# A fused streaming-encoder block on eight cores: the constant matmuls at the opening taken out, and the last tile's residual added on VectorE

## What is computed

```
h    = rms_norm(x, ln_mix_pre)
B, C, u, v = split(h @ w_in)                       # 2048 -> 4096
y_a  = per-head-norm(B * conv3_causal(C * u))      # 1024 channels
y_b  = per-group-norm(pool(v) @ pool_w) * scale    # 1024 channels
x    = x + rms_norm(concat(y_a, y_b) @ w_out, ln_mix_post)
hf   = rms_norm(x, ln_ffn_pre)
ff   = (silu(hf @ w_gate) * (hf @ w_up)) @ w_down  # 2048 -> 5632 -> 2048
out  = x + rms_norm(ff, ln_ffn_post)
```

## Time and profile before

| | us |
|---|---|
| median of three runs | 2515.8 |
| the three runs | 2512.62, 2515.8, 2649.74 |
| the profiled execution, its own time | 2530.27 |
| its span on the slowest core (core 1) | 2528.7 |
| spans of the eight cores | 2506.2 to 2528.7 |

### The profile page before, as it was taken

How to read it: one execution, slowest core, us unless ns; L and a number is a source line. 1 busy time by engine, 2 the same in 40 slices (tenths; PEclk the granted TensorE clock), 3 DMA queues, 4 the chain that set the end, 5 groups by cost and what they waited for, 6 DMA issues and landing times.

```text
span 2528.7 us, 31891 instructions; the slowest of 8 cores (2506.2 to 2528.7 us)
## 1 busy us (share of the span) xinstructions
PE 2460.2 (97%) x11570; PEld 1110.1 (44%) x11570; DVE 1056.3 (42%) x1614; ACT 641.0 (25%) x1184; POOL 219.0 (9%) x373
## 2 busy tenths in 40 slices
PE   6999999999999999999999999999999999999994
PEld 2444444444444444444444444444444444444441
DVE  4445627544445543322235552654545445200202
ACT  3222334222222222311123333432222222111110
POOL 0000000000000000002101000000000000000212
PEclk7889999999999999999999999999999999999997
DMA  8859768988998998776987524896554445344664
GB/s 214 162 77 126 144 197 219 187 137 126 135 134 127 134 134 215 243 231 183 256 148 112 96 84 167 225 193 116 91 92 84 84 88 92 129 150 150 182 194 66
DMA packets 75339, 374.53 MB, mean 148 GB/s; under 512 B 8240, under 2 KB 10544, under 8 KB 45872
## 3 DMA queue, kind: packets, MB, share of 16 engines
q0 software_dynamic: 54160, 313.55, 62.4%
q1 hardware_dynamic: 21024, 58.94, 7.3%
HBM read 509.82 MB, written 65.01 MB: 227 GB/s over the span
## 4 chain that ended last, share of the span: by engine, by line
PE 94%; DMA 3%; DVE 2%; issue 0%; SPq 0%; POOL 0%; ACT 0%; DVEq 0%; POOLq 0%; ACTq 0%
PE bank L409 92%; DMA unit<-wst_gu 1%; PE bank L600 1%; DMA F<-xt 1%; PE bank L449 1%; PE bank L872 1%; DMA unit<-wst_in 0%; DVE XG L444 0%; DVE unit L441 0%; PE bank L401 0%; DVE XG L441 0%; SPq L499 0%; PE bank L531 0%; POOL yT L1118 0%; DVE F L444 0%
## 5 line engine op out<-in xcount | busy, mean ns | idle before, releaser
L409 PE MATMUL bank<-XG,unit 128*128 128x512 bf16 x7680 | 1698.9, 383 | 11.5 <-DMA unit<-wst_in 6.7
L409 PEld LDWEIGHTS bank<-XG,unit 128*128 128x128 bf16 x7680 | 756.3, 99 | 937.4 <-issue 88.0
L409 PE MATMUL bank<-F,unit 128*128 128x512 bf16 x3072 | 669.2, 379 | 0.0
L409 PEld LDWEIGHTS bank<-F,unit 128*128 128x128 bf16 x3072 | 300.6, 98 | 362.4
L441 DVE TENSOR_TENSOR tt<-tt 128x512 f32<-128x512 f32 (+1 forms) x152 | 104.9, 691 | 597.8 <-ACT tt L438 576.8
L435 ACT ACTIVATE tt<-bank 128x512 f32<-128x512 f32 x228 | 136.2, 597 | 481.5 <-PE bank L409 474.8
L441 DVE TENSOR_TENSOR bank<-bank,tt 128x512 f32<-128x512 f32 x152 | 106.3, 699 | 357.5 <-PE bank L409 357.5
L438 ACT ACTIVATE tt<-bank 128x512 bf16<-128x512 f32 (+1 forms) x160 | 95.0, 595 | 492.7 <-PE bank L409 483.8
L441 DVE TENSOR_TENSOR unit<-unit 128x1024 bf16<-128x1024 bf16 x304 | 196.1, 686 | 10.4 <-PE bank L409 2.1
L441 DVE TENSOR_TENSOR F<-bank,tt 128x512 bf16<-128x512 f32 x138 | 95.2, 691 | 118.2 <-PE bank L409 97.3
L357 POOL DMA_DIRECT2D unit<-wst_gu x100 | 52.9, 529 | 1016.8 <-PE bank L409 913.0
(11 more groups left out here) (74 smaller groups left out, 874.3 us busy)
## 6 DMA issues: line engine op xcount, KB each, us to landing
unit<-wst_gu POOLq DMA_DIRECT2D x100, 1024.0 KB, 10.6
unit<-wd_bf POOLq DMA_DIRECT2D x64, 1024.0 KB, 5.5
unit<-wo_bf POOLq DMA_DIRECT2D x32, 1024.0 KB, 6.5
unit<-wst_in POOLq DMA_DIRECT2D x31, 1024.0 KB, 12.0
unit<-wd_bf POOLq DMA_DIRECT2D x32, 768.0 KB, 6.6
wd_bf<-wst_dn POOLq DMA_DIRECT2D x32, 704.0 KB, 15.8
tt<-xt SPq DMA_DIRECT2D x64, 256.0 KB, 6.2
yT<-XG POOLq DMA_DIRECT2D x56, 256.0 KB, 9.6
```

Of the source, the lines that this page charges most:

```text
L409: inst = e.matmul(out, lhsT=pairs[n][0], rhs=pairs[n][1], start=(start and n == 0), stop=(stop and n == nk - 1), skip_group_check=lax)
```

## The change

Opening: the memset of `tt8` and the 24 matmuls are gone. End, for the last tile only: `dn_tile` gets `apart=True`, with which `Acc` closes its running sum at the fifteenth square and leaves the sixteenth out of it; `rsqrt` sums both over partitions, with two matmuls into one bank. Items 0 to 5 stay as they were. Items 6 to 15 are done by the new `item_here`: VectorE scales the chunk and adds x to it, and SP stores the sum with a plain transfer. For this x after the mixing is read back from `yT` into F0, chunks 6 to 15, in five pieces.

```diff
         class Acc:
-            def __init__(self, n, tile=2, home=None):
-                self.n, self.i, self.tile, self.home = n, 0, tile, home
+            def __init__(self, n, tile=2, home=None, apart=False):
+                self.n, self.i, self.tile, self.home, self.apart = n, 0, tile, home, apart
+                self.last = None
...
                 q = self.q
-                if self.i < self.n:
+                if self.apart and self.i == self.n:
+                    self.last = q
+                    return
+                if self.i < self.n - self.apart:
                     tt(Tt[self.tile][:], Tt[self.tile][:], sqv(q), ALU.add, [self.h, q], [self.h])
...
             def rsqrt(self, n, out, hout):
                 b = next_bank()
-                P.op("pe", lambda e: e.matmul(banks[b.i][:], lhsT=ones[:], rhs=self.outv(), start=True, stop=True),
+                P.op("pe", lambda e: e.matmul(banks[b.i][:], lhsT=ones[:], rhs=self.outv(), start=True, stop=self.last is None),
                      reads=[self.out, "ones"], writes=[b])
+                if self.last is not None:
+                    stat_mm(b, self.last, False, True)
                 rsqrt_to(b, n, out, hout)
...
+            def item_here(self, i):
+                t = self.t
+                p = t % 2
+                stt(ffv(p, i), ffv(p, i), C_G3 + i, Tt[3][:], Kff(p, i) + [self.h], Kff(p, i))
+                tt(xs(i), ffv(p, i), xs(i), ALU.add, Kff(p, i) + Kx(i), Kx(i))
+                P.dma("sp", lambda e: e.dma_start(out=yT[t][:, i, :], in_=xs(i)).then_inc(sems[f"oh{i}"], 16),
+                      f"oh{i}", reads=Kx(i), writes=[("y", t, i)])
...
-        P.op("dve", lambda e: e.memset(Tt[8][:], 0.0), writes=[("sq", 2), ("sq", 3)])
...
-        warm = next_bank()
-        for i in range(24):
-            P.op("pe", lambda e: e.matmul(banks[warm.i][:], lhsT=ones[:], rhs=Tt[8][:].bitcast(BF16)[:, 0:TT], start=True, stop=True),
-                 reads=["ones", ("sq", 2)], writes=[warm])
...
+                if c2 == 3 and p == 1:
+                    for n in range(3, 8):
+                        P.dma("sp", lambda e, n=n: e.dma_start(out=xs2(n), in_=yT[to][:, 2 * n:2 * n + 2, :]).then_inc(sems[f"xl{n}"], 16),
+                              f"xl{n}", reads=[("y", to, 2 * n), ("y", to, 2 * n + 1)], writes=Kx2(n))
...
-            acc = dn_tile(1, side_d1)
+            acc = dn_tile(1, side_d1, p == 1)
             tail = Tail(to, acc)
 
         tail.rs3()
-        for i in range(KC):
+        for i in range(6):
             tail.item(i)
-        names = [f"o{q}" for q in range(16)] + [f"{x}{q}" for x in ("xo", "xp") for q in range(8)]
+        for i in range(6, KC):
+            tail.item_here(i)
+        names = [f"o{q}" for q in range(16)] + [f"oh{q}" for q in range(6, 16)] + [f"{x}{q}" for x in ("xo", "xp") for q in range(8)]
         P.wait_all("sp", [(q, P.dma_cnt[q]) for q in names])
```

More of the change, by code:

```diff
@@ L151, in build_program @@
     sem_names = (list(ENGS) + [f"u{i}" for i in range(5)] + [f"xl{i}" for i in range(8)] + [f"xm{i}" for i in range(8)] + [f"xp{i}" for i in range(8)]
-                 + [f"xo{i}" for i in range(8)] + [f"o{i}" for i in range(16)] + ["ua0", "ua1", "ua2", "ua3", "misc", "pw", "xhl", "st4", "st5", "st6", "st9", "st7", "rs0", "rs1"]
+                 + [f"xo{i}" for i in range(8)] + [f"o{i}" for i in range(16)] + ["ua0", "ua1", "ua2", "ua3", "oh6", "oh7", "oh8", "oh9", "oh10", "oh11", "oh12", "oh13", "oh14", "oh15", "misc", "pw", "xhl", "st4", "st5", "st6", "st9", "st7", "rs0", "rs1"]
                  + [f"cv{i}" for i in range(4)])
@@ L1074, in gu_fast, with dn_tile @@
                 side(n)
-        def dn_tile(par, side):
-            acc = Acc(KC)
+        def dn_tile(par, side, apart=False):
+            acc = Acc(KC, apart=apart)
             pend = []
```

## The result

The changed kernel's median is 2498.5 us (2497.5 to 2500.4, four runs). The two runs of the kernel before that they are compared with took 2512.6 and 2515.8 us; the ratio is 0.9938, 95% interval 0.9914 to 0.9962.

A forecast was written before the change was run, and what follows sets the result against it. The kernel was taken as matmul-filled, its end bound by transfers, then by VectorE; opening 0, end -9.5 us (0.8 from the last sum included) and reload 0 gave 2506.3 us from the 2515.8 us median, range 2500 to 2521 us.

The forecast's parts named there:

- Opening: 0: Opening: removing the memset and 24 constant matmuls changes nothing, because the weight transfer covers any slower start; 0 us.
- The rule that the prediction cites against the change: Opening: the Trainium skill says TensorE's clock is throttled by default and activity releases it, so the phase would start at half speed.
- all-cold bound: Opening: with the clock at 1.2 GHz throughout, the first phase ends at 34.2 us; core 1 loses nothing, core 0 0.7 us.
- Rival (b): Opening: it stays cold into the next phase; up to 5 us lost where cover fails, 2507 to 2511 us; chance 0.10.
- Rival (c): Opening: slow matmuls leave PE no gap, so the clock is up afterwards; gain about 2 us, 2504 us; chance 0.06.
- The last sum: 0.8 us: End: the last square in its own matmul takes VectorE's add and hand-over off the chain; 0.8 us saved.
- That is 1.53 us an item and 15.3 us for ten.: End: VectorE's scale and dependent add for items 6 to 15, so VectorE ends 7.8 us later than before.
- 2.3 us remain for SP's last waits and the end of the program: End: time from the last landing, at about 2526.4 us, to the end of the old span at 2528.7 us.
- The transfers as not the bound (17.0 against VectorE's 19.3 us): End: six accumulating transfers at 1.66 us and ten stores at 0.70 us, together 17.0 us, finish before VectorE's path.
- Rival (a): End: plain stores are as dear as accumulating transfers; only 0.8 us saved, 2515.0 us; chance 0.08.
- Rival (d): End: VectorE's ten scale-and-add pairs are slow; at 3.06 us an item 5.8 us slower, 2521.6 us; chance 0.03.
- Rival (e): Whole program: saving as forecast, but the median falls on an execution with the 0.81 clock; 2520.8 us; chance 0.11.

The follow-up runs named there:

- e10: The full change measured again beside the kernel before: 2499.0 us against 2512.3 us, ratio 0.9952.
- e1: Only the opening edit (memset and 24 constant matmuls removed) on the kernel before, with its old end: 2512.9 us against 2512.3 us, ratio 0.9993.
- e8: The full change plus 20 extra matmuls in PE's wait for the second weight unit: 2498.4 us, the kernel before 2513.0 us.
- e7: The full change with the order turned round, ten VectorE items first and six accumulating ones last: 2508.2 us against 2513.0 us for the kernel before.
- e12: The full change with each of the ten scales issued one item ahead: 2502.8 us against 2513.6 us for the kernel before, ratio 0.9952.

## Why the prediction was wrong, point by point

The mechanism was right and two sizes were off. The saving at the end was forecast as 9.5 us and is 11.9 us. The base to carry it to was 2515.8 us, and the kernel before runs at 2512.3 us. With both put right the forecast would have been 2500.4 us instead of 2506.3 us; 2498.5 to 2499.0 us is measured. Of the last 1.4 to 1.9 us, 0.5 us is that the slowest core stands less above the mean (e10); the rest is open.

- **Opening: 0.** Right, by the reason given: e1's mean span is that of before within 0.2 us, and the weight unit ends PE's wait. The rule that the prediction cites against the change is borne out too: without the constant matmuls the first pair takes 1.06 us on every core. With them it took 0.59 us on seven of eight cores of before, so core 1, from which the prediction argued, was the exception. The all-cold bound wasn't reached on any core of e1; the latest end of the phase was 32.3 us, against the bound's 34.2 us. Rival (b) falls with it. Rival (c), a clock that is up behind the wait, did not come by itself, and brought about on purpose (e8) it gave no gain clear of the spread.
- **The last sum: 0.8 us.** Measured 0.9 us in the start of the first scale (2.63 against 3.55 us), since the matmul follows the square by 0.14 us and not 0.25 us. At the old end it would have been worth 0.5 to 0.8 us.
- **"That is 1.53 us an item and 15.3 us for ten."** VectorE took 18.98 us from first scale to end, forecast 19.3: 0.35 us off. Half of the items took 1.46 us.
- **"The shortest landing of a plain store of 512 KB is 2.6 us."** The last one of 256 KB landed in 2.0 us. 0.6 us off; I had taken the larger store's for the smaller one.
- **"2.3 us remain for SP's last waits and the end of the program": within the saving, the step that failed most.** I carried it over unchanged. After the change it is 0.9 us, 1.4 us less. I had read it as a fixed cost of the program's end; e7 shows that it is longer when accumulating transfers come last (1.8 us). What lengthens it, the accumulation or POOL's queue, stays open. The four add up: 0.1 + 0.35 + 0.6 + 1.4 = 2.4 us, which is 11.9 - 9.5.
- **The transfers as not the bound (17.0 against VectorE's 19.3 us).** Right in its outcome and closer than I thought: measured prices are 1.77 and 0.72 us, 17.8 us in all, and e12 shows them as an equal bound. (My 1.66 us was elapsed time by item, and 26.9 us over sixteen is 1.68 us; by the same reading as here it is 1.80 us in the kernel before.) Rival (a) falls: a plain store costs 40% of an accumulating transfer here. Rival (d) falls: an item never took over 1.6 us.
- **The reload: 0.** Right. It was issued from 2314.8 us, 12 us before the end of the even tile's down projection and so earlier than forecast, and PE had no wait for weights behind it.
- **Carrying to the median.** The median of three runs, one of them at 2649.74 us, was the higher of the other two. In the later measurements before's medians were 2512.3, 2513.0 and 2513.6 us. The range's low end was built from 2512.6 us, 9.5 us and 2.4 us for (c), which the text of (c) puts at about 2 us. With 11.9 us in place of 9.5 us it would have been 2498.3 us, just below the measured 2498.5 us, so the undersized saving broke it. Rival (e) is real but rare: the profiled execution of the earlier trace rows and two of some sixty more runs of the kernel before took 2530 to 2535 us, with a lowest mean clock of 0.976 to 0.978.

## What to carry to other kernels

Where a program ends on accumulating transfers, one of them can cost more than twice a plain store (1.77 against 0.72 us here), and the close behind them is longer (1.8 to 2.3 us against 0.9 us); if an engine is idle by then and the addend can be fetched early, add there and store plainly. Split the items so that the adding engine and the transfers end together: here six to ten was that point, and moving it by two cost 1.5 to 2 us on either side. A warm-up on constant data can speed up the first matmuls and still be worth nothing, if a transfer ends the wait behind them: here they made the first pairs 0.47 us shorter, and the time didn't change.

## What the runs showed that I had not expected

- The end of the program costs 0.9 us behind the last plain store and 1.8 to 2.3 us behind the last accumulating transfer.
- A float32 add of 128x512 on VectorE takes 1.50 us instead of 0.69 us beside POOL's, which takes 1.57 us itself.
- The column of the granted clock read 1.00 from 12 to 15 us while pairs of matmuls took 1.06 us, as they do where it reads 0.50. Here the matmuls' own times show the clock there, and the column doesn't.
- Adjacent dependent VectorE steps cost 0.1 to 0.17 us of gap; issuing the scale one item ahead took an item from 1.46 to 1.53 us down to 1.27 us.
